# A two-layer trunk on one core: one weight matrix per head for both scan directions of the second mixer, with the time steps in the masked state products

## The reference, cut to what matters

```python
xdt = _chunks((xs * dt[..., None]).reshape(b, l, g, k, p), L)
a = _chunks((dt * A).reshape(b, l, g, k), L)
...
cs = jnp.cumsum(ac, axis=1)
seg = jnp.where(lower, cs[:, :, None] - cs[:, None, :], -jnp.inf)
w = jnp.einsum('blgn,bsgn->blsg', cc, bc)[..., None] * jnp.exp(seg)
y = jnp.einsum('blsgk,bsgkp->blgkp', w, xc)
y = y + jnp.einsum('blgn,bgkpn->blgkp', cc, state) * jnp.exp(cs)[..., None]
```

## Time and profile before

| | us |
|---|---|
| median of 3 runs | 2180.51 (2179.99 to 2181.98) |
| the profiled execution | 2181.06 |
| span of its core | 2179.4 |
| granted TensorE clock, mean | 0.979 of full speed |

### The profile page before, as it was taken

One profiled execution on the slowest core, in us unless ns is written; L12 is line 12 of the kernel. 1 busy time (PEld: TensorE's weight loads), 2 busy tenths in 40 slices (PEclk: granted clock), 3 DMA queues, 4 the chain that ended last, 5 costly groups with the idle time before them and its releaser, 6 DMA issues.

```text
span 2179.4 us, 31194 instructions
## 1 busy us (share of the span) xinstructions
PE 2056.1 (94%) x10686; PEld 1697.1 (78%) x10686; DVE 1432.1 (66%) x1841; ACT 919.7 (42%) x1267; POOL 755.1 (35%) x687
## 2 busy tenths in 40 slices
PE   4898999999999999969988999999999999999997
PEld 2466788888888888757876888888888888887776
DVE  2236777777777777854239777776777676678344
ACT  3234544445454554524335343343344434336333
POOL 0025656666656555632113223122223222222011
PEclk9899999999999999989999999999999999999999
DMA  7985666666666666543442545545554645545653
GB/s 267 357 240 142 170 164 172 174 180 171 176 173 180 176 167 166 157 116 102 135 140 62 143 126 157 140 125 130 144 137 113 159 115 145 135 119 175 232 193 135
DMA packets 417743, 349.20 MB, mean 160 GB/s; under 512 B 13504, under 2 KB 358176, under 8 KB 416544
## 3 DMA queue, kind: packets, MB, share of 16 engines
q1 hardware_dynamic: 392016, 267.67, 42.7%
q0 software_dynamic: 20400, 74.46, 13.6%
q10 hardware_dynamic: 5280, 6.47, 0.9%
HBM read 344.21 MB, written 4.33 MB: 160 GB/s over the span
## 4 chain that ended last, share of the span: by engine, by line
PE 77%; DVE 7%; DMA 4%; issue 4%; ACT 3%; POOL 3%; SPq 1%; POOLq 0%; DVEq 0%; ACTq 0%
PE bank L351 19%; PE bank L353 19%; PE bank L355 19%; DMA arena<-in_na_ada_w_dram 3%; PE bank L1995 2%; PE bank L2065 2%; PE bank L2067 2%; PE bank L2066 2%; POOL acc L575 2%; DVE w_lo L337 2%; PE bank L1978 1%; PE bank L1988 1%; DVE act_lo L1490 1%; PE bank L1763 1%; DVE arena L1515 1%
## 5 line engine op out<-in xcount | busy, mean ns | idle before, releaser
L351 PE MATMUL bank<-act_hi,w_hi 128*128 128x512 f32 (+1 forms) x2480 | 919.2, 371 | 34.7 <-DVE w_lo L337 25.0
L353 PE MATMUL bank<-act_lo,w_hi 128*128 128x512 f32 (+1 forms) x2480 | 902.7, 364 | 0.0
L355 PE MATMUL bank<-act_hi,w_lo 128*128 128x512 f32 (+1 forms) x2480 | 902.1, 364 | 0.0
L337 DVE TENSOR_TENSOR w_lo<-arena,w_hi 128x2048 fp32r<-128x2048 f32 x186 | 440.4, 2368 | 205.5 <-ACT w_hi L333 144.3
L351 PEld LDWEIGHTS bank<-act_hi,w_hi 128*128 128x128 f32 x2480 | 471.8, 190 | 115.4 <-DVE w_lo L337 23.5
L355 PEld LDWEIGHTS bank<-act_hi,w_lo 128*128 128x128 f32 x2480 | 471.3, 190 | 74.4
L353 PEld LDWEIGHTS bank<-act_lo,w_hi 128*128 128x128 f32 x2480 | 472.3, 190 | 69.7
L575 POOL TENSOR_TENSOR acc<-acc,arena 128x512 f32<-128x512 f32 x224 | 319.1, 1425 | 130.5 <-ACT arena L817 121.2
L333 ACT ACTIVATE w_hi<-arena 128x2048 fp32r<-128x2048 f32 x141 | 269.2, 1909 | 99.8 <-PE bank L2067 79.5
L1294 DVE SCALAR_TENSOR_TENSOR arena<-arena,cond_c 128x512 f32<-128x512 f32 x240 | 258.8, 1078 | 75.4 <-DMA arena<-in_ssd_ada_w_dram 43.5
L817 ACT ACTIVATE arena<-arena,cond_c 128x512 f32<-128x512 f32 x256 | 171.5, 720 | 295.9 <-POOL acc L575 176.4
(11 more groups left out here) (245 smaller groups left out, 2090.6 us busy)
## 6 DMA issues: line engine op xcount, KB each, us to landing
arena<-in_ssd_w_in_dram SPq DMA_DIRECT2D x81, 1024.0 KB, 5.8
arena<-in_na_w_in_dram SPq DMA_DIRECT2D x58, 1024.0 KB, 7.2
arena<-in_ssd_ada_w_dram POOLq DMA_DIRECT2D x96, 512.0 KB, 4.0
arena<-in_na_ada_w_dram SPq DMA_DIRECT2D x64, 512.0 KB, 8.3
arena<-in_ssd_w_out_dram SPq DMA_DIRECT2D x32, 1024.0 KB, 5.1
arena<-in_na_ada_w_dram POOLq DMA_DIRECT2D x32, 512.0 KB, 4.1
arena<-in_na_w_out_dram SPq DMA_DIRECT2D x16, 1024.0 KB, 6.2
arena<-cs_scr SPq DMA_DIRECT2D x64, 256.0 KB, 5.4
```

Of the source, the lines that this page charges most:

```text
L337: nc.vector.tensor_tensor(w_lo[:, n0 % 2, :], raw[slot], w_hi[:, n0 % 2, :].bitcast(F32), ALU.subtract).then_inc(s_lo, 1)
L351: nc.tensor.matmul(bank[b][:, 0:cols], w_hi[:, b, w], act_hi3[:, k, 0:cols], start=(k == 0), stop=False)
L353: nc.tensor.matmul(bank[b][:, 0:cols], w_hi[:, b, w], act_lo3[:, k, 0:cols], start=False, stop=False)
L355: mm = nc.tensor.matmul(bank[b][:, 0:cols], w_lo[:, b, w], act_hi3[:, k, 0:cols], start=False, stop=(k == KT - 1))
```

## The change

PE multiplies the unweighted tokens by one 256 x 256 matrix for each head, in which both directions are added. The time steps of the tokens go into a second matrix `w_cb`, and `decay` is multiplied by it in place.

- `x_weighted` copies the latent tokens as they are to `x_lt` and weights only the context tokens (they still feed the states).
- ACT's new `cb_by_dt` writes `w_cb`, four instructions of 256 columns: row block `st` of `cb_m` times the time steps of one direction (forward for the first 128 tokens, backward for the last). It waits for the mix of the pair before, which reads `w_cb`.
- DVE's new `cb_diagonals` adds the other direction's triangle on the two diagonal blocks of each head, four instructions of 128 columns.
- POOL's `make_mix` is one instruction of 1024 columns, and waits for the exponential and for `cb_diagonals`.
- PE's `products` has four matmuls of 256 columns in the place of eight.
- `decay_args` waits for the products of the pair before (PE), no longer for its mix (POOL), since `decay` is now what PE reads.
- One semaphore stands where `s_sp_pace` and `s_pool_pace` did. Nothing waits for any of them.

Where the new steps stand in the order: ACT has `cb_by_dt(j)` behind the convolution's tanh of pair j (ahead of z's tanh) for j > 0, and behind the exponential for j = 0. DVE has `cb_diagonals(j)` behind `decay_args(j)` for j > 0. That of pair 0 stands one pair later, between the weight split and the last step of the convolution of pair 1.

```diff
-            def make_mix(pair, turn, group):
+            def make_mix(pair, turn):
 
                 pool.wait_ge(s_exp2, turn.at(pair + 1))
-                if pair > 0 or turn.i is not None or turn.base:
-                    pool.wait_ge(s_y3, turn.at(pair))
-                pool.wait_ge(s_cbm, group)
-                for at, size, st, l0 in ((0, 256, 0, 0), (512, 128, 1, 128), (768, 256, 1, 0), (1280, 128, 0, 0)):
...
-                last.then_inc(s_mix, 1)
+                pool.wait_ge(s_wcb, turn.at(pair + 1))
+                flat = decay.rearrange("p h s l -> p (h s l)")
+                nc.gpsimd.tensor_tensor(flat, flat, w_cb.rearrange("p h s l -> p (h s l)"), ALU.mult)\
+                  .then_inc(s_mix, 1)
...
+            def cb_by_dt(p, t1, t4):
+
+                act.wait_ge(s_cbm, t1.at(1))
+                if t4.i is not None or p > 0:
+                    act.wait_ge(s_mix, t4.at(p))
+                else:
+                    act.wait_ge(s_fev, 2)
+                for hd in range(2):
+                    for st in range(2):
+                        at = 2 * p + 64 * st + hd
...
+                        last = nc.scalar.activation(w_cb[:, hd, st, :], cb_m[:, 384 * st:384 * st + LAT], ACT.Copy,
+                                                    scale=dt)
+                last.then_inc(s_wdt, 1)
...
                     conv_tanh(2 + j, t6)
+                    if j > 0:
+                        cb_by_dt(j, t1, t4)
                     if j < PAIRS - 1:
                         z_tanh_s(j, t10)
...
-                        if j > 0:
+                        if j == 0:
+                            cb_by_dt(0, t1, t4)
+                        else:
                             square(j - 1, t4)
...
-                src = bank[2][:, :].rearrange("p (t h d) -> p t h d", t=4, h=2)
+                nc.vector.tensor_copy(x_lt.rearrange("p t d -> p (t d)"), bank[2][:, 0:2 * P])
+                src = bank[2][:, 2 * P:4 * P].rearrange("p (t h d) -> p t h d", t=2, h=2)
...
-                    dve.wait_ge(s_mix, t4.at(p))
+                    dve.wait_ge(s_y3, t4.at(p))
...
+            def cb_diagonals(p, t4):
+
+                dve.wait_ge(s_wdt, t4.at(p + 1))
+                for hd in range(2):
+                    for st, at in ((0, 640), (1, 256)):
+                        w = w_cb[:, hd, st, P * st:P * st + P]
+                        m = nc.vector.scalar_tensor_tensor(
+                            w, cb_m[:, at:at + P], f_tok[:, st, heads_at(p, t4, 64 * (1 - st) + hd, 1)], w,
+                            ALU.mult, ALU.add)
+                m.then_inc(s_wcb, 1)
...
+                    def between(j=j):
+                        lo_s(4 + 2 * j, t10)
+                        if j == 1:
+                            cb_diagonals(0, t4)
+
+                    conv(2 + 2 * j, 2 + j, j, 4, t10, t6, between, x_c, x_free)
...
                         decay_args(j, t4)
+                        if j > 0:
+                            cb_diagonals(j, t4)
...
-                for n, (d, st, at, l0, size) in enumerate(((0, 0, 0, 0, 256), (0, 1, 512, 128, 128),
-                                                           (1, 1, 768, 0, 256), (1, 0, 1280, 0, 128))):
+                for st in range(2):
                     for hd in range(2):
...
+                        mm = nc.tensor.matmul(bank[5][64 * hd:64 * hd + 64, 0:LAT], x_lt[:, st, 64 * hd:64 * hd + 64],
+                                              decay[:, hd, st, :], start=(st == 0), stop=(st == 1),
+                                              skip_group_check=True)
                 mm.then_inc(s_y3, 1)
```

More of the change, by code:

```diff
@@ L202, in trunk @@
         decay = region(24, 2, 2, LAT)
-        mix = region(28, 6 * LAT)
+        w_cb = region(28, 2, 2, LAT)
         inter = region(34, 2 * LAT)
@@ L212, in trunk @@
         x_c = region(78.25, 2, LAT)
-        xdt = region(80.25, 2, 4, P)
+        x_lt = region(80.25, 2, P)
+        xdt = region(81.25, 2, 2, P)
         state = region(84.25, 2 * P)
@@ L304, in trunk @@
         s_sqs, s_acs = sem("y_square"), sem("y_acc")
+        s_wdt, s_wcb = sem("cb_by_dt"), sem("cb_weights_ready")
         s_yhi, s_ylo = sem("y_hi_ready"), sem("y_lo_ready")
@@ L552, in load_ada @@
                 if i is not None:
-                    pool.sem_inc(s_pool_pace, 1)
+                    pool.sem_inc(s_pace, 1)
                 if gate:
@@ L706, in _ @@
                 group_steps(i, False)
-            make_mix(31, Turn(), GROUPS)
+            make_mix(31, Turn())
             add_square(30, Turn())
@@ L1645, in ssd_group @@
                     decay_args(-1, t4)
+                    cb_diagonals(-1, t4)
                 conv(0, 0, 32, 1, t10, t6, lambda: lo_s(2, t10), b_t, none)
@@ L1715, in _ @@
                         decay_args(-1, end)
+                        cb_diagonals(-1, end)
                     if m == 0 and q == 5:
@@ L1977, in states @@
                 for t in range(2):
-                    mm = nc.tensor.matmul(bank[3][:, 0:2 * P], b_tok[:, t, :], xdt[:, :, 2 + t, :],
+                    mm = nc.tensor.matmul(bank[3][:, 0:2 * P], b_tok[:, t, :], xdt[:, :, t, :],
                                           start=(t == 0), stop=(t == 1))
@@ L1990, in products @@
                 pe.wait_ge(s_mix, t4.at(p + 1))
-                for n, (d, st, at, l0, size) in enumerate(((0, 0, 0, 0, 256), (0, 1, 512, 128, 128),
-                                                           (1, 1, 768, 0, 256), (1, 0, 1280, 0, 128))):
+                for st in range(2):
                     for hd in range(2):
-                        mm = nc.tensor.matmul(bank[5][64 * hd:64 * hd + 64, l0:l0 + size],
-                                              xdt[:, d, st, 64 * hd:64 * hd + 64],
-                                              mix[:, at + hd * size:at + (hd + 1) * size],
-                                              start=(n == 0), stop=(n == 3), skip_group_check=True)
+                        mm = nc.tensor.matmul(bank[5][64 * hd:64 * hd + 64, 0:LAT], x_lt[:, st, 64 * hd:64 * hd + 64],
+                                              decay[:, hd, st, :], start=(st == 0), stop=(st == 1),
+                                              skip_group_check=True)
                 mm.then_inc(s_y3, 1)
```

18 lines of the change are left out of this document (7 added, 11 removed).

## The result

The changed kernel takes 2219.74 us (median of 4, 2216.67 to 2221.44), the kernel before 2180.45 (median of 4, 2179.99 to 2181.98). The ratio is 1.0179, with a 95% interval from 1.0166 to 1.0192: 39.3 us slower, where 24.9 were forecast. The direction holds, but the time is above the upper end of the range, 2216.

What follows compares the result with a forecast made beforehand. The mixer was taken to be bound by PE's own work. Terms of -15.0 (saving), +25.3 (wait), +12.0 (clock), +0.8 (convolution) and +1.8 (behind the mixer) give +24.9 us on 2180.51: 2205.4 us, range 2193 to 2216.

Steps and rivals of the forecast that it cites:

- The bound and the place: In the mixer PE's own work bounds; PE would stand ahead of pair 0's products in every group, waiting for POOL's mix.
- the saving: PE's products, four in place of eight: 0.99 us against 1.46, 0.47 us a pair, -15.0 us over 32 pairs.
- The wait: PE ahead of pair 0's products: 3.2 us in seven groups and 2.9 in group 0, +25.3 us.
- the 0.45 kept for it: POOL's mix slowed by running beside DVE's convolution: up to 0.45 us each, 3.6 us more in the sum.
- The list of idle times: PE's clock fell behind idle times of 2.83, 2.91, 3.04 and 3.73 us and stayed up behind 1.97.
- and then DVE has caught up: Pair 1: z's tanh, weight split and DVE's combine come some 5.5 us late, covered by the next x tile's 11 us.
- its term for the clock: Behind each of PE's eight waits the clock falls to 1.2 GHz, costing 1.5 us each, +12.0 us.
- a term that was set at nothing: ACT held by `cb_by_dt(1)` in pair 1, with DVE some 5.5 us late behind it: no cost in the sum.
- The margin that "just closes": ACT in pairs 1 and 2, with the copies ahead of z's tanh: 0.67 us to spare against 0.7 late.
- The rival "longer": Longer wait and wake, with ACT and DVE late in pairs 1 and 2: up to +39.7 us, 2220; chance 0.10.
- Behind the mixer: First output tiles: ACT's copies put 0.7 us and `cb_diagonals(31)` 1.1 us on DVE's path, +1.8 us.

Runs made afterwards that it cites:

- e1: The changed kernel with pair 0's `cb_diagonals` right behind its own exponents, ahead of pair 1's convolution steps on DVE: 2180.08 us, ratio 0.9997.
- e9: The changed kernel run once more without any edit, for a comparison on one chip: 2220.80 us, ratio 1.0189.
- e3: The changed kernel with PE kept busy by 13 unused multiplications of 512 columns while it waits for pair 0's mix: 2217.31 us, ratio 1.0172.
- e2: The changed kernel with pair 0's diagonals early and `cb_by_dt` of pairs 1 to 3 behind z's weight split on ACT: 2172.38 us, ratio 0.9963.
- e7: The changed kernel with early diagonals, late copies and, in pair 0, the convolution's last step ahead of DVE's weight split: 2176.28 us, ratio 0.9979.
- e8: The changed kernel with `cb_by_dt` behind z's weight split on ACT and pair 0's diagonals still late: 2208.27 us, ratio 1.0126.

## Why the prediction was right and wrong

**What held.** The bound and the place: PE stands ahead of pair 0's products in each of the eight groups, released by POOL, and e1 takes it away. `cb_diagonals` took 1.13 us (1.14 forecast). Four products take 1.02 us where nothing disturbs them (in group 0 from 1269.81 to 1270.83), 0.99 forecast, so the saving is 0.44 and not 0.47 a pair. The wait is 27.7 us in all, 25.3 forecast; 0.27 of each comes from POOL's 2.66 us beside the end of the convolution against 2.38 alone (2.39 forecast), inside the 0.45 kept for it. An uncovered low clock costs 1.45 to 1.6 us (1.5 forecast), and seven of eight waits had a low clock behind them (all eight in e9). The list of idle times behind this was not complete: in the kernel before PE also stood for 2.17 us up to 934.72 with the clock at 1.00 behind it, and for 1.82 us up to 1136.18 with 0.50 behind it, so 1.97 was not the longest that left the clock up. The forecast does not hang on it.

**The step that failed: "and then DVE has caught up".** The prediction said that ACT, held by `cb_by_dt(1)`, and DVE behind it are some 5.5 us late in pair 1, and that the next x tile and the low clock cover it. The rows: pair 1's exponential (ACT L1014) stands 11.8 us behind PE's transposes (1345.20 against 1333.38). Before, it stood 9.1 behind them:

```profile
1335.56 1.06 ACT L1017 ACTIVATE arena<-arena 128x1024 f32<-128x1024 f32 x1 [8.62 <-DVE arena L1566]
```

and PE's were at 1326.46. The 2.7 us left are more than ACT's 1.14 of slack and the convolution's 0.40 together can take, and PE waits for the convolution at pair 2. The prediction set the 5.5 us against the length of an x tile, at no cost in the sum. What counts is how far PE was held itself, 3.1 us net, and those two slacks, which stood in its own rows.

**Two terms that overlap were added or left out.** Without the low clock a group would have taken 104.80 us (e3), 4.16 above before; the forecast without its term for the clock was 1.46. e3 less e2, step by step, splits this: 3.44 for the wait, 1.75 for the hold-up (0.33 of it the place of the copies), 0.48 more for where the copies stand, less the 1.51 that e2 gains. The low clock then adds at most 2.4 to 3.7 us in the whole kernel in the place of 12, since PE would have waited in most of that time anyway. So a term that was set at nothing was worth 7 x 1.75 us and 1.2 in group 0, some 13 us (11 without the copies' place), and one that was right by itself fell by at least 8 to 10. By place, the profiled span is 15.5 us above the forecast: 8.2 of it lie in groups 1 to 6 (4.32 against 2.96 each), 0.3 in group 0, 6.0 from group 7 to the end and 0.9 ahead.

**The margin that "just closes".** Pairs 2 and 3 were to save 0.42 and 0.47 us each; over groups 1 to 6 they saved 0.22 and 0.28. The four copies take 1.70 us, not 1.3: they do not overlap, 0.4 each. ACT is then late by more than its margin of 0.67, and PE waits 0.25 us for the convolution, as in e1. In e2, where the copies stand behind the weight split, these steps are 0.45 and 0.39 us shorter than before. The rival "longer" had named this, for pairs 1 and 2.

**Behind the mixer: +1.8 forecast.** Steps of group 7 and the way from there to the end took 10.7 us more, where some 4.7 were forecast. ACT's timeline of the changed kernel where it splits the weights of the first output tile, for which it waits for their load:

```profile
2002.07 1.91 ACT L335 ACTIVATE w_hi<-arena 128x2048 fp32r<-128x2048 f32 x1 [4.27 <-DMA arena<-in_ssd_w_out_dram]
```

The same in the kernel before:

```profile
1965.94 1.92 ACT L333 ACTIVATE w_hi<-arena 128x2048 fp32r<-128x2048 f32 x1 [2.35 <-DMA arena<-in_ssd_w_out_dram]
```

And in e2:

```profile
1953.79 1.92 ACT L335 ACTIVATE w_hi<-arena 128x2048 fp32r<-128x2048 f32 x1 [2.50 <-DMA arena<-in_ssd_w_out_dram]
```

SP issues this load behind those of the running sums, which wait for DVE's combine of pair 1 (L1616), and this stands on DVE behind the weight split for the next z, ahead of which the copies of pair 2 have come: 9.66 us behind the transposes of pair 2 against 8.17 before. The load and all behind it come later, and PE waits at the output tiles of the changed kernel (its timeline):

```profile
2016.47 0.71 PE L2100 MATMUL bank<-w_hi,act_hi 128*128 128x512 f32 x1 [3.01 <-DVE act_lo L1741]
...
2075.82 0.80 PE L2100 MATMUL bank<-w_hi,act_hi 128*128 128x512 f32 x1 [4.34 <-DVE w_lo L339]
```

The first was 1.97 us before, with the clock at 1.00; at 3.01 it is followed by 3.5 us at 0.51. The second was 2.91. The prediction counted the copies and the diagonals on DVE's way and not the transfer that hangs on the moved split.

The copies' place is a part of the excess and not all of it. The load is issued 9.67 us behind pair 2's transposes in e1 and e3, and 8.60 in e2, e7 and e8, where the copies stand late; the first of the two output tiles starts 9.50 us behind pair 3's transposes in the former and 8.17 in the latter (8.21 before). So the place costs 1.3 us there. But e7 and e8 take 212.5 and 212.3 us for the way to the end, as e1 does (212.1), and only e2 takes 209.4. The stretches behind PE's next wait of this kind, 1.87 us long in e2 and 1.88 in e8, columns as above:

```profile
1974.50:1978.50 4.00, 4.00 (x18) 3.29 (x19) 4.00 (x5) 3.46 (x8) 2.36 (x1) 1.00 0.01 4
2013.90:2017.90 4.00, 4.00 (x11) 3.15 (x12) 4.00 (x5) 3.45 (x8) 2.37 (x1) 0.57 0.00 1
```

The clock stayed up in one and fell in the other, and PE comes to the third wait 1.5 us later in e8. The load's own time differs too: from issue until ACT goes on 6.8 us in e2 and 8.5 in e7, and the step 2 to 3 of group 7 takes 20.26 and 22.04. How the 6 us divide between the copies, the load and the clock stays open: there is one profile for each kernel.

## What to carry over

Ask of a moved small step who waits for its result, and then who waits for that: the result was late for PE by 3.5 us, but the second waiter, ACT, cost another 1.4 because its queue held the next tile's work. A slow clock of an engine and a wait that follows for engines that are late themselves don't add up: here the longer of the two set the step in most groups. An engine that is 0.4 us from being the bound takes back most of what another one saves, so its path is part of any saving's price.

## What the hardware showed

- POOL's multiplication and DVE's subtraction of two stored operands (128 x 2048) ran one after the other: DVE took 4.10 us and not 2.29 when it came second. POOL's pair of instructions took 4.86 us and not 2.53 when it was split around DVE's. The second case is one that splitting an instruction made worse.
- Idle times of PE of 3.1 to 3.5 us were followed by 1.2 GHz in seven of eight groups of the changed kernel and in six of eight in e8. The Trainium skill (TensorE: Matmul & The Clock Gate, HAM oscillation) tells of an array that waits once a pass and runs slowly after each wait; here that was so after most. In e9, the same kernel as the changed one, it was so after all eight. What made the others differ was not tested. Length alone does not tell: behind the mixer 1.88 us in e8 were followed by a clock of 0.57, 1.87 in e2 by 1.00, and 2.96 us in e1 (up to 1973.12) by 1.00.
